# First projection: two blocks of 512 columns taken together, x in quarters, and the last squares summed on VectorE

## What is computed

```python
def rmsnorm(x, g):
    xf = x.astype(jnp.float32)
    y = xf * lax.rsqrt(jnp.mean(xf * xf, axis=-1, keepdims=True) + NORM_EPS) * g.astype(jnp.float32)
    return y.astype(x.dtype)

# first_block, its beginning
h = rmsnorm(x, norm_mix[layer])
(q, kc, vc, ks, vs, kw, vw, nsa_g, rq, rk, rv, rg, gate_a, gate_b) = jnp.split(
    h @ w_in[layer], offsets, axis=-1)          # w_in: 1024 x 5400
...
# second_block, its end
h = h + swiglu(rmsnorm_2(h, norm_ffn[i]), w_ffn_in[i], w_ffn_out[i])
return rmsnorm_2(h, norm_final)
```

## Time and profile before

| | us |
|---|---|
| three runs, median (lowest to highest) | 963.6 (963.57 to 964.12) |
| the profiled execution, its own time | 963.97 |
| its span, first to last instruction | 962.0 |
| PE busy in it | 953.4 |
| DMA orders: first 128 tokens of x, second 128, tile 0, tile 3 | 0.74, 1.18, 1.64, 4.05 |
| first matmul of the projection | 7.82 |
| start of block 2 | 31.39 |
| start of the last matmul | 955.62 |

### The profile page before, as it was taken

How to read it: one execution, slowest core, us unless ns; L and a number is a source line. 1 busy time by engine, 2 the same in 40 slices (tenths; PEclk the granted TensorE clock), 3 DMA queues, 4 the chain that set the end, 5 groups by cost and what they waited for, 6 DMA issues and landing times.

```text
span 962.0 us, 16219 instructions
## 1 busy us (share of the span) xinstructions
PE 953.4 (99%) x6674; PEld 861.6 (90%) x6674; DVE 634.6 (66%) x824; ACT 520.2 (54%) x790; POOL 62.7 (7%) x113
## 2 busy tenths in 40 slices
PE   9999999999999999999999999999999999999997
PEld 7877889989988888989977999998998899999996
DVE  5778685777555555778857787776666466555554
ACT  5577554555444444566865674545555445444443
POOL 3100001001000000314000001100000010000001
PEclk9999999999999999999999999999999999999999
DMA  9974436456655656556464455455655346665661
GB/s 306 313 238 129 146 88 177 157 173 206 199 187 178 194 177 197 154 179 194 141 193 136 129 174 199 157 189 165 202 164 172 113 154 219 184 202 170 196 190 45
DMA packets 133545, 170.39 MB, mean 177 GB/s; under 512 B 5824, under 2 KB 97296, under 8 KB 133472
## 3 DMA queue, kind: packets, MB, share of 16 engines
q1 hardware_dynamic: 131408, 165.07, 54.3%
q10 hardware_dynamic: 1424, 2.84, 0.9%
q0 software_dynamic: 640, 1.44, 0.6%
HBM read 168.28 MB, written 1.05 MB: 176 GB/s over the span
## 4 chain that ended last, share of the span: by engine, by line
PE 90%; DVE 5%; ACT 2%; issue 1%; DMA 1%; POOL 0%; POOLq 0%; DVEq 0%; ACTq 0%
PE ps L374 13%; PE ps L375 13%; PE ps L376 13%; PE ps L405 8%; PE ps L406 8%; PE ps L407 8%; PE ps L740 5%; PE ps L739 5%; PE ps L738 5%; PE ps L357 4%; PE ps L461 3%; DVE parts L1564 2%; DVE room L1598 1%; PE ps L492 1%; PE ps L493 1%
## 5 line engine op out<-in xcount | busy, mean ns | idle before, releaser
L1564 DVE TENSOR_TENSOR parts<-raws,parts 128x1024 fp32r<-128x1024 f32 (+2 forms) x307 | 367.5, 1213 | 220.2 <-ACT parts L1041 219.7
L1041 ACT ACTIVATE parts<-raws 128x1024 fp32r<-128x1024 f32 (+2 forms) x307 | 315.7, 1045 | 233.7 <-PE ps L376 131.5
L374 PE MATMUL ps<-room_r,parts 128*128 128x256 f32 x1248 | 351.9, 282 | 0.1
L375 PE MATMUL ps<-room_r,parts 128*128 128x256 f32 x1248 | 348.9, 280 | 0.0
L376 PE MATMUL ps<-room_r,parts 128*128 128x256 f32 x1248 | 348.4, 279 | 0.0
L374 PEld LDWEIGHTS ps<-room_r,parts 128*128 128x128 f32 x1248 | 234.6, 188 | 6.1 <-issue 4.3
L375 PEld LDWEIGHTS ps<-room_r,parts 128*128 128x128 f32 x1248 | 234.6, 188 | 1.3
L376 PEld LDWEIGHTS ps<-room_r,parts 128*128 128x128 f32 x1248 | 234.7, 188 | 0.0
L405 PE MATMUL ps<-parts,room_r 128*128 128x512 f32 (+1 forms) x336 | 134.4, 400 | 1.3 <-DVE parts L1564 1.3
L407 PE MATMUL ps<-parts,room_r 128*128 128x512 f32 (+1 forms) x336 | 131.1, 390 | 0.0
L406 PE MATMUL ps<-parts,room_r 128*128 128x512 f32 (+1 forms) x336 | 131.1, 390 | 0.0
(11 more groups left out here) (226 smaller groups left out, 877.3 us busy)
## 6 DMA issues: line engine op xcount, KB each, us to landing
raws<-in_w_in SPq DMA_DIRECT2D x99, 512.0 KB, 4.5
raws<-in_w_ffn_in SPq DMA_DIRECT2D x44, 512.0 KB, 4.0
raws<-in_w_up SPq DMA_DIRECT2D x32, 512.0 KB, 4.4
raws<-in_w_down SPq DMA_DIRECT2D x32, 512.0 KB, 4.1
raws<-in_w_ffn_out SPq DMA_DIRECT2D x22, 512.0 KB, 4.1
raws<-in_w_xkv SPq DMA_DIRECT2D x16, 512.0 KB, 3.7
raws<-in_w_out SPq DMA_DIRECT2D x8, 512.0 KB, 4.2
raws<-in_w_up_ssd SPq DMA_DIRECT2D x8, 512.0 KB, 5.1
```

The source lines that it names most:

```text
L374: e.matmul(ps, wh, hT[0][:, k, :], start=k == 0, stop=False)
L375: e.matmul(ps, wh, hT[1][:, k, :], start=False, stop=False)
L1041: e.activation(t.h, t.raw, ACT.Copy).then_inc(s["hi"], 1)
L1564: e.tensor_tensor(t.l, t.raw, t.h.bitcast(F32), ALU.subtract).then_inc(s["lo"], 1)
```

## The change

In the first projection, blocks 0 and 1 of 512 columns are taken together, in four banks of their own (`first_two`): the order of weight tiles is block 0 with slices 0, 1, 2, 3 in tiles of depth 1, block 1 with slices 0 to 3 in two tiles of depth 2, then block 0 with slices 4 to 7, then block 1 with slices 4 to 7. That is ten tiles instead of nine. x comes in quarters and halves of the features for all 256 tokens: SP orders the first quarter at the very start, the second after tile 1, the second half after tile 3. ACT's queue orders all the columns (77 KB) and then ident. PE turns slice by slice, two transposes into a bank, two slices after the first load, two after tile 0, four after tile 4. ACT rounds each slice straight out of its bank with the gain as scale, and DVE takes the rest from the bank in one instruction; `gains` is no longer used there. The sums of squares on ACT move behind tile 6. At the end DVE squares and sums the last 256 columns itself, starting from the sum of the other parts, which POOL has prepared; POOL then only takes the power.

```diff
-            def x_half(q):
-                for t in range(2):
-                    need(s[f"x{t}{q}"], 16)
-                    turn_x(MIX, t, q)
+            def x_quarter(q, *loads):
+                for load in loads:
+                    need(s[load], 16)
+                for k in (2 * q, 2 * q + 1):
+                    turn(("turn", MIX, k), [x[:, t, P * k:P * k + P] for t in range(2)])
 
             idle(6)
-            x_half(0)
+            x_quarter(0, "x_first")
             idle(5)
 
+            def first_two(w, hT, ready):
+                own = [[bank(), bank()] for _ in range(2)]
+                for blk, k0, depths in ((0, 0, (1, 1, 1, 1)), (1, 0, (2, 2)), (0, 4, (2, 2)), (1, 4, (2, 2))):
+                    for deep in depths:
+                        w_ = weight(w[k0 * P:(k0 + deep) * P, 512 * blk:512 * blk + 512], deep, 512)
+                        need(s["lo"], w_.i + 1)
+                        k1 = k0 + deep
+                        for t in range(2):
+                            ps, tok = psum[:, own[blk][t], :], slice(t * P, t * P + P)
+                            for k in range(k0, k1):
+                                ready(k)
+                                wh, wl = w_.h[:, k - k0, :], w_.l[:, k - k0, :]
+                                e.matmul(ps, hT[0][:, k, tok], wh, start=k == 0, stop=False)
+                                e.matmul(ps, hT[0][:, k, tok], wl, start=False, stop=False)
+                                last = e.matmul(ps, hT[1][:, k, tok], wh, start=False, stop=k == 7)
...
-            units = tm("qkv", w_in, 0, 512, xT, x_ready(MIX), depths=[1, 1, 2, 2, 2])
+            units = first_two(w_in, xT, first_ready)
             next(units)
-            next(units)
-            x_half(1)
+            x_quarter(1, "x_second")
+            for _ in range(4):
+                next(units)
+            x_quarter(2, "x01", "x11")
+            x_quarter(3)
             run(units)
-            run(tm("qkv", w_in, 0, 1304, xT, x_ready(MIX), first=1))
+            run(tm("qkv", w_in, 0, 1304, xT, first_ready, first=2))
...
-            e.dma_start(x[:, 0, 0:512], xin[:, 0, 0:512]).then_inc(s["x00"], 16)
-            e.dma_start(cols[:, 0:8], a["cols"][:, 0:8]).then_inc(s["gain"], 16)
+            e.dma_start(cols[:, :], a["cols"]).then_inc(s["cols"], 16)
+            e.dma_start(ident, a["ident"]).then_inc(s["ident"], 16)
...
+            def first_rounds(*ks):
+                for k in ks:
+                    e.wait_ge(s["pe"], where["turn", MIX, k].at)
+                    e.activation(xT[0][:, k, :], psum[:, where["turn", MIX, k].bank, 0:256], ACT.Copy,
+                                 scale=col("norm_mix")[:, k:k + 1]).then_inc(s["first_hi"], 1)
...
+            first_rounds(0)
             round_tile()
-            rounds(MIX, 0, True, (1,))
+            first_rounds(1)
             round_tile()
             round_tile()
-            e.dma_start(cols[:, 8:], a["cols"][:, 8:]).then_inc(s["cols"], 16)
+            first_rounds(2, 3)
             round_tile()
-            rounds(MIX, 1, True)
             round_tile()
+            round_tile()
+            first_rounds(4, 5, 6, 7)
+            round_tile()
+            settle()
...
-            e.activation(junk[:, 768:D], x[:, 1, 768:D], ACT.Square, accum_out=sum_D, scale=1 / 32).then_inc(s["sumsq"], 1)
...
+            def first_rests(*ks):
+                for k in ks:
+                    name = ("turn", MIX, k)
+                    e.wait_ge(s["first_hi"], k + 1)
+                    emptied(stt(xT[1][:, k, :], bank_of(name)[:, 0:256], col("norm_mix")[:, k:k + 1],
+                                xT[0][:, k, :].bitcast(F32), ALU.mult, ALU.subtract), name)
...
+            out_of("last")
+            e.wait_ge(s["before"], 1)
+            e.tensor_tensor_reduce(junk[:, 768:D], rest_, rest_, 1 / D, last_sums[2], ALU.mult, ALU.add, sum_D).then_inc(s["last_sum"], 1)
...
-            step(e.tensor_tensor(before_D, of[1][1], before_1, ALU.add))
-            settle()
-            e.wait_ge(s["sumsq"], n + 5)
-            r = rstd[sq_of["final"]][1]
-            step(e.tensor_tensor(r, sum_D, before_D, ALU.add))
-            settle()
-            e.tensor_tensor(r, r, half[:, 0:1], ALU.pow).then_inc(s["rstd"], 1)
+            e.tensor_tensor(before_D, of[1][1], before_1, ALU.add).then_inc(s["before"], 1)
+            e.wait_ge(s["last_sum"], 1)
+            e.tensor_tensor(rstd[sq_of["final"]][1], sum_D, half[:, 0:1], ALU.pow).then_inc(s["rstd"], 1)
...
-            e.dma_start(ident, a["ident"]).then_inc(s["ident"], 16)
-            e.dma_start(x[:, 1, 0:512], xin[:, 1, 0:512]).then_inc(s["x10"], 16)
-
-            w1_behind = {7: 0, 9: 1, 11: 2, 12: 3, 17: 4, 18: 5, 19: 6, 21: 7}
+            e.dma_start(x[:, :, 0:256], xin[:, :, 0:256]).then_inc(s["x_first"], 16)
+
+            w1_behind = {8: 0, 10: 1, 12: 2, 13: 3, 18: 4, 19: 5, 20: 6, 22: 7}
...
-                if t.i == 2:
+                if t.i == 1:
+                    e.dma_start(x[:, :, 256:512], xin[:, :, 256:512]).then_inc(s["x_second"], 16)
+                if t.i == 3:
                     for half_ in range(2):
                         e.dma_start(x[:, half_, 512:], xin[:, half_, 512:]).then_inc(s[f"x{half_}1"], 16)
```

More of the change, by code:

```diff
@@ L36 @@
 SEMS = (
-    "x00", "x01", "x10", "x11", "gain", "ident", "consts", "decay", "cols", "rows", "pos", "w1k", "w1v", "w2k", "w2v", "wa2", "mem", "out",
+    "x_first", "x_second", "x01", "x11", "ident", "consts", "decay", "cols", "rows", "pos", "w1k", "w1v", "w2k", "w2v", "wa2", "mem", "out",
     "pe", "hi", "lo",
     "act_step", "dve_step", "pool_step",
-    "final_col", "gain2", "sumsq", "zsq", "rstd", "z", "zrstd", "mlp_rstd", "x_scale", "spread", "xT_hi", "xT", "y",
+    "final_col", "gain2", "sumsq", "zsq", "rstd", "z", "zrstd", "mlp_rstd", "x_scale", "spread", "first_hi", "xT_hi", "xT", "y",
     "zeros", "red", "trig", "q_rot", "r_rot", "gsig", "again", "no_keys", "win_end", "windows", "pc_sub", "pc_exp", "pc", "nmax", "weighed",
@@ L51 @@
     "klast", "khexp", "kh", "dec", "e2", "r", "o_sum", "o_rstd", "o_out", "oT2_hi", "oT2",
-    "px_max", "px", "mk_hi", "mk_lo", "mv_hi", "qx_hi", "pxT_hi", "ox_hi", "last_row", "last_sum", "out_act", "out_rows",
+    "px_max", "px", "mk_hi", "mk_lo", "mv_hi", "qx_hi", "pxT_hi", "ox_hi", "last_row", "before", "last_sum", "out_act", "out_rows",
 )
@@ L522, in x_ready, with first_ready @@
             def x_ready(u):
-                return lambda k, t=1: need(s["xT"], 4 * u + (1 if k < 4 else 3) + t)
+                return lambda k, t=1: need(s["xT"], 4 * (u - 1) + (1 if k < 4 else 3) + t)
+            def first_ready(k, t=1):
+                out_of(("turn", MIX, k))
             def mixed_ready(u):
@@ L543, in tensor @@
             idle(5)
+            def first_two(w, hT, ready):
[13 more added lines that the diff above has]
+                                last = e.matmul(ps, hT[1][:, k, tok], wh, start=False, stop=k == 7)
+                            if k1 == 8:
+                                ends(last, ("qkv", blk, t), own[blk][t])
+                        w_.release = count if k1 == 8 else done(last)
+                        k0 = k1
+                        yield
@@ L552, in tensor @@
             spread_rstd(2, MIX)
-            fill = chain(*(tm(name, w_in, c0, 512, xT, x_ready(MIX), True)
+            fill = chain(*(tm(name, w_in, c0, 512, xT, first_ready, True)
                            for name, c0 in (("rq", 1304), ("rk", 1816), ("rg", 2840), ("rv", 2328))),
-                         fm("sig", w_in, 3352, 2048, xT, x_ready(MIX)))
+                         fm("sig", w_in, 3352, 2048, xT, first_ready))
             step(4)
@@ L1139, in scaled @@
                 return rstd[sq_of[u]][t]
-            rounds(MIX, 0, True, (0,))
+            def first_rounds(*ks):
[3 more added lines that the diff above has]
+                                 scale=col("norm_mix")[:, k:k + 1]).then_inc(s["first_hi"], 1)
+            e.wait_ge(s["zeros"], 1)
+            step(e.activation(junk[:, P:P + 1], junk[:, 0:1], ACT.Copy))
+            e.wait_ge(s["cols"], 16)
+            first_rounds(0)
             round_tile()
-            rounds(MIX, 0, True, (1,))
+            first_rounds(1)
             round_tile()
             round_tile()
-            e.dma_start(cols[:, 8:], a["cols"][:, 8:]).then_inc(s["cols"], 16)
+            first_rounds(2, 3)
             round_tile()
-            rounds(MIX, 1, True)
             round_tile()
+            round_tile()
+            first_rounds(4, 5, 6, 7)
+            round_tile()
+            settle()
+            for load in ("x_first", "x_second", "x01"):
+                e.wait_ge(s[load], 16)
             for q in range(2):
-                e.wait_ge(s[f"x0{q}"], 16)
                 sum_of(x, 0, q, MIX)
@@ L1156, in scalar @@
             e.dma_start(consts[:, 0:early], a["consts"][:, 0:early]).then_inc(s["consts"], 16)
+            e.wait_ge(s["x11"], 16)
```

(20 more changed lines are left out.)

3 lines of the change are left out of this document (removed).

## The result

The changed kernel takes **965.04 us** (median of 22 runs, 964.28 to 966.58); the kernel before, run beside it, 963.83 (22 runs, 963.18 to 965.05). The forecast was 964.0 in a range from 962.6 to 965.4. The time is in the range; the way to it is in good part another, and most of this text is about that.

A forecast was written before the change was run, and what follows sets the result against it. PE, busy 99% of the span, bounds the kernel, so only start and tail can win. Head +0.7 and tail -0.3 give +0.4: 964.4 against the profiled 963.97, 964.0 against the median 963.6; range 962.6 to 965.4.

The forecast's parts named there:

- First inputs: Head: first x, columns and ident, 397 KB travelling together, land at 4.06 (bounds 3.84 and 4.58).
- First matmul at 6.5: Head: first projection matmul starts at 6.5, 1.3 us earlier than before, with the gain multiplication off the path.
- The clock rises late: Rival, head: a hole before the first transposes delays PE's full clock, 3.1 us on top, 967.1; chance 0.06.
- Tile 4 takes the gain back: First projection: weight tile 4 lands at 11.55; PE waits 1.4 us and starts it at 14.0 (bound 12.55).
- The wait before tile 6: First projection: tile 6 stands behind four roundings on ACT, so PE waits 0.3 us (bounds 0 and 0.6).
- The angles end late: Rival: tile 13 landing after 33 delays angles and sines; PE waits up to 1 us near 38.5, 964.9; chance 0.11.
- The tail: After the last matmul: DVE's summing instruction replaces ACT's square, its read and POOL's addition; 0.3 us won.
- The sum: Whole kernel: head +0.7 and tail -0.3 give +0.4 us, 964.0 against the median.
- the signs that the prediction set itself: Wrong in main step if tile 4 meets no wait; wrong altogether with new holes beyond 32 or 0.25 us transposes beyond 6.

The follow-up runs named there:

- e1: Changed kernel with ident ordered ahead of the columns on ACT's queue: 964.36 us, 1.0008 of the kernel before.
- e4: Changed kernel with nine instead of six idle matmuls (18 passes, not 12) ahead of the first transposes: 964.75 us, 1.0011 of the kernel before.
- e5: Changed kernel with ident first on SP's queue, x first on ACT's, the gain's 8 columns behind it, the other columns later: 964.63 us.
- e6: e5 with weight tile 6 split ahead of the four roundings of x's second half: 963.67 us, 0.9997 of the kernel before.
- e8: e6 with x's second half ordered after tile 4 instead of tile 3: 963.13 us, 0.9992 of the kernel before.
- e7: Changed kernel with only tile 6 split ahead of the four roundings of x's second half, loads left alone: 964.29 us, 1.0008 of the kernel before.
- e3: Changed kernel with the old end (ACT squares the last 256 columns): 965.99 us, 1.0026 of the kernel before.
- e10: e9 with the third and fourth compression-weight pieces ordered behind tiles 15 and 16 instead of 12 and 13: 962.25 us, 0.9987 of the kernel before.
- e9: e8 with tile 7 also split ahead of the first two sums of squares on ACT: 963.27 us, 0.9998 of the kernel before.

## Why the prediction was right, and where it was not

- **First inputs: wrong.** The step that failed is "397 KB: between 3.84 and 4.58 in proportion, 4.06". It took three transfers as one. x (4.43) and the columns (4.2) lie in its bounds; ident does not (5.3): it is ordered 0.48 later because ACT orders it second, and lands 4.1 us after that. The prediction weighed the Trainium skill's rule that every DMA engine takes turns between queues (DMA: Bandwidth & Descriptors, section on queues, rings and completion order); the trace agrees in that the packets of x and of the columns run side by side, from 1.8 to 3.9 and from 2.1 to 3.7 us. (That x took 3.7 us to land, against 3.1, does not test the rule: before, it had ident and the other x beside it.) What decided was not x beside the columns; it was ident behind them in one queue. e1 shows it by the swap.
- **First matmul at 6.5: wrong, 8.36.** Of the 1.86, the lower clock level makes 0.33 (e4, with the pace restored, has 8.03), ident's place about 1.05 (e1, with the two swapped, has 6.98), and 0.48 are there even with ident early: the columns, second on ACT's queue, then let the first rounding start at 4.9 to 5.2, where the forecast had it at 4.67. The chain from there to the matmul was sized right: 1.83 forecast, 1.8 measured, though a rounding takes 0.47 us, not the 0.38 of the plain copy that was its nearest row.
- **"The clock rises late": it came in part.** The rival named the condition, a hole before the first transposes, and gave it 0.06. The hole came, from ident, and the price of its mechanism was 0.9 in the profiles (e4), not 3.1 on top: PE rose at about 9.7, after tile 0's first matmuls, and not only after tile 1.
- **Tile 4 takes the gain back: not in after, but right as a mechanism.** The forecast start was 14.0. e4 has it at 14.18 without any wait, since its start is late; e5 at 13.72 and e6 at 14.14, with waits of 0.43 and 0.99; e8 removes the wait by its stated cause. The landing, forecast at 11.55 with 10.1 as the other bound, came at 11.0 in e1, 11.3 in e5 and 11.7 in e6. So the lag was there, and after lacks only the early start that it would have eaten.
- **The wait before tile 6: right**, 0.42 where 0.3 was said, in every kernel that keeps the order (the four roundings, put at 1.35 without a row, took 1.44: 18.29 to 19.73 on ACT); with its surroundings it costs 0.7.
- **"The angles end late": it came, nearly as told.** Tile 13 landed at 33.3 in after, beyond the 33 of the rival, behind a piece of the compression weights, and pushed the sines, which ended at 37.4; tile 14, late behind the pieces too, added 0.5. PE waited 0.48 at 40.42, where the rival had up to 1 us at 38.5. In e7 tile 13 and the sines alone make the wait (0.84), in e8 (0.85) and e4 (0.22) both do. It is not there in every run: e3, whose head is that of after, has tile 13 at 32.7 and no wait. e10, with the pieces behind the tiles, has both tiles early and no wait. The rival had a chance of 0.11.
- **The tail: right.** 0.41 won where 0.3 was said: 0.48 for the sum and 0.08 for reading it out, the two-input form that was taken as nearest, without ACT's 0.19.
- **The sum.** Forecast +0.7 and -0.3; measured in the profiles +2.2 (at the end) and -0.41, in the medians +1.2 in all. That the time fell into the range was luck in good part: the upper end, 965.4, stood there for the late angles, which made 0.5 to 0.7 of the loss, and late ident and clock, which it was not meant for, made the rest. By the signs that the prediction set itself it was wrong altogether: PE meets tile 4 without waiting, a new hole opens beyond 32 (at 40.42), and the transposes still run at the lower pace beyond 6 (5.48 to 6.36). The missing 2.0 us at 40 us are 1.1 at tile 4 (late ident and clock), 0.2 at tile 6, and 0.7 in front of the next projection (0.48 of it the wait for tile 14, which the late tile 13 began).

## What to carry to other kernels

When several small inputs release the first instruction, follow each to its landing by its own queue and place in it, and not their bytes as one sum: here the second order on ACT's queue landed about 1 us (0.8 to 1.2) after the first, with 4, 64 or 77 KB, and that, with the slow passes behind it, turned a forecast gain of 1.3 us at the first matmul into a loss of 0.5. Ask of every hole at the start of a busy engine what pace it has afterwards, and look at the durations, since the page's clock line can miss it. A start that is made earlier is only kept if the next wait in the list, and the one behind it, are moved as well: here tiles 4 and 6, and tiles 13 and 14, each took their share.

## What the runs showed that was not expected

- The moment at which PE reaches the upper level moves between runs even where the start is the same. e8, e9 and e10 have the same instructions up to 7 us, and on PE, ACT and DVE so has e6; in e6, e8, e9 and e10 the ten idle passes took 1.74, 2.09, 1.28 and 1.28 us. e5, with hardly a hole before its transposes (4.09, idle passes until 3.97), still had 2.24. The Trainium skill (TensorE: Matmul & The Clock Gate, part 1) says that the release of the clock is variable from run to run; these rows agree. The granted clock of the profile reads 1.00 in each of these stretches.
- A transfer of 4 KB (the gain's 8 columns in e5), second on ACT's queue behind 256 KB of x, took 3.7 us to land, and one of 64 KB 2.6 when it was first on SP's:

```profile
x<-in_x ACTq DMA_DIRECT2D x1, 256.0 KB, 3.3
...
ident<-in_ident SPq DMA_DIRECT2D x1, 64.0 KB, 2.6
cols<-in_cols ACTq DMA_DIRECT2D x1, 4.0 KB, 3.7
```

- The summing instruction of DVE appears in the trace as two, 0.48 us for 256 columns and 0.08 for the sum.
